# Expert outputs of the first token block brought forward into the input stage, with a weight table for each token block and four places for v's halves

## The reference

```
q = x @ wq; s1, s2 = q_half1 . subkeys1, q_half2 . subkeys2
v1, i1 = top_k(s1, 16);  v2, i2 = top_k(s2, 16)
vals, pos = top_k(v1[:, None] + v2[None, :], 16)
ids = i1[pos // 16] * 128 + i2[pos % 16];  g = softmax(vals)
a = x . u_tab[ids];  y = sum over heads and k of gelu(a) * g * v_tab[ids]
x = LayerNorm(alpha * x + y)
```

## Time and profile before

| | |
|---|---|
| runs (3) | 1092.28 to 1094.7 us, median 1093.67 |
| the profiled execution | 1090.26 us |
| its span | 1088.3 us |
| PE busy | 1021.7 us (94%), 6826 instructions |
| DVE / ACT / POOL busy | 838.3 (77%) / 451.0 (41%) / 451.5 (41%) us |
| DMA | 210.41 MB, 193 GB/s over the span |

### The profile page before, as it was taken

The page is one execution under the profiler, slowest core; times in us unless marked ns, Lnnn a source line. Parts: engine busy times, 40 slices in busy tenths (PEclk is TensorE's granted clock), DMA queues, the critical chain, the costliest instruction groups (busy, mean ns, idle before and its releaser), DMA issues.

```text
span 1088.3 us, 20500 instructions
## 1 busy us (share of the span) xinstructions
PE 1021.7 (94%) x6826; PEld 937.8 (86%) x6826; DVE 838.3 (77%) x1484; ACT 451.0 (41%) x648; POOL 451.5 (41%) x332
## 2 busy tenths in 40 slices
PE   7999999899999999999999999139999999999995
PEld 7878898899999999999999999128888888888884
DVE  3476457778999998988888887038888888888887
ACT  4374444344443334444444444014444444444442
POOL 5800000058888888788888888830000000000000
PEclk9999999999999999999999999559999999999998
DMA  9676688545666667877787775247777777777773
GB/s 305 240 271 224 208 294 295 180 117 117 141 145 141 136 136 164 195 167 170 164 174 168 170 172 99 0 125 238 243 241 241 240 242 240 241 241 241 240 240 128
DMA packets 146735, 210.41 MB, mean 193 GB/s; under 512 B 47376, under 2 KB 95312, under 8 KB 146704
## 3 DMA queue, kind: packets, MB, share of 16 engines
q1 hardware_dynamic: 109264, 208.58, 61.0%
q0 software_dynamic: 37440, 1.43, 10.1%
HBM read 192.00 MB, written 17.96 MB: 193 GB/s over the span
## 4 chain that ended last, share of the span: by engine, by line
PE 47%; POOL 38%; issue 8%; DVE 3%; DMA 2%; ACT 1%; SPq 0%; POOLq 0%; DVEq 0%; ACTq 0%
POOL expert_weights L459 38%; PE ps L1283 32%; PE ps L1200 13%; DMA w_raw<-in_w_in_dram 1%; DVE w_lo L904 1%; ACT w_hi L577 1%; PE ps L1096 1%; PE ps L1074 1%; DVE xres L703 0%; DVE xres L710 0%; PE ps L1084 0%; DMA expert_weights<-gw,cell 0%; DVE small L691 0%; DVE v_lo L984 0%; PE ps L1107 0%
## 5 line engine op out<-in xcount | busy, mean ns | idle before, releaser
L459 POOL DMA_INDIRECT expert_weights<-gw,cell x256 | 411.8, 1609 | 256.4 <-DVE gw L897 175.8
L1241 PE MATMUL ps<-act_hi,uT_hi 128*128 128x256 f32 x1024 | 295.1, 288 | 0.0
L1241 PE MATMUL ps<-act_hi,uT_lo 128*128 128x256 f32 x1024 | 289.9, 283 | 0.0
L1241 PE MATMUL ps<-act_lo,uT_hi 128*128 128x256 f32 x1024 | 289.7, 283 | 0.0
L657 ACT ACTIVATE v_hi<-v_raw 128x512 fp32r<-128x512 f32 x256 | 147.9, 626 | 244.3 <-PE ps L1283 198.5
L1283 PE MATMUL ps<-v_hi,hid_hi 128*128 128x512 f32 x512 | 158.8, 391 | 43.8 <-DVE v_lo L984 43.8
L1241 PEld LDWEIGHTS ps<-act_lo,uT_hi 128*128 128x128 f32 x1024 | 196.6, 192 | 0.0
L1241 PEld LDWEIGHTS ps<-act_hi,uT_hi 128*128 128x128 f32 x1024 | 196.6, 192 | 0.0
L1241 PEld LDWEIGHTS ps<-act_hi,uT_lo 128*128 128x128 f32 x1024 | 196.3, 192 | 0.0
L984 DVE TENSOR_TENSOR v_lo<-v_raw,v_hi 128x512 fp32r<-128x512 f32 x256 | 165.0, 686 | 0.0
L1283 PE MATMUL ps<-v_hi,hid_lo 128*128 128x512 f32 x512 | 158.1, 390 | 0.0
(11 more groups left out here) (151 smaller groups left out, 1397.9 us busy)
## 6 DMA issues: line engine op xcount, KB each, us to landing
v_raw<-in_peer_v_dram SPq DMA_DIRECT2D x128, 512.0 KB, 4.2
u_raw<-in_peer_u_dram SPq DMA_DIRECT2D x68, 512.0 KB
u_raw<-in_peer_u_dram SPq DMA_DIRECT2D x240, 128.0 KB
w_raw<-in_w_in_dram SPq DMA_DIRECT2D x8, 2048.0 KB, 9.5
...
g_in<-expert_weights SPq DMA_DIRECT2D x128, 128.0 KB, 3.0
w_raw<-in_peer_wq_dram SPq DMA_DIRECT2D x4, 2048.0 KB, 10.6
...
```

The lines of the kernel that those rows point to most:

```text
L459: pool.indirect_dma_start(out=table_cells, out_offset=bass.IndirectOffsetOnAxis(ap=cell[:, t, k:k + 1], axis=0), in_=gw[:, t, k:k + 1], in ...
L1241: ins = pe.matmul(ps[:, bank, 0:T], (uT_hi, uT_hi, uT_lo)[part][:, slot, k, :], (act_hi, act_lo, act_hi)[part][:, k, :], start=(k == 0 and ...
```

## The change

- The table is stored as two tables, one for each token block, each with 128 columns. `column` carries the offset of the second. A gate load of both token blocks now reads 256 rows of 512 bytes, where before it read 128 rows of 1 KB.
- The last routing batch (heads 4 to 7) is split into heads 4 and 5, and heads 6 and 7.
- POOL's scatters follow `ORDER`: token block 0 is brought forward, with 4 scatters of token block 1 between its heads (8 after head 7), and then heads 3 to 7 of token block 1 follow each other directly. The rule on earlier heads is unchanged.
- In input rounds 10 to 17 PE adds, after each of the first three blocks' inputs, the token block 0 outputs of one of the expert blocks 104 to 127 (a "fill"): two float32 matmuls of 512 columns, without a split. SP loads its gates (64 KB) and v (512 KB), from round 10 on, after it has waited for all scatters of token block 0. DVE multiplies the gates by H.
- In the output stage the blocks stand in 32 groups of four. In 24 of them the fourth block is one of 104 to 127, for token block 1 alone (6 matmuls, and `hidden` on 128 columns). The other 8 groups are whole. The v of a filled block is loaded a second time.
- `v_hi` and `v_lo` have four places. DVE does `rest_v` two blocks ahead: after `hidden` of block m comes `rest_v` of m + 2, and `rest_v` of blocks 0 and 1 comes ahead of `hidden` of block 0. ACT's rounding waits for block m - 4. SP's order is unchanged: after `hid_done` of m the gates of m + 2, then the v of m + 4.

The diff, cut to its core:

```diff
@@ -36,6 +36,12 @@
 GROUP = 4
 ROUNDS = (NB - NPRE) // GROUP
 BODY = 4
+AHEAD = 2
+FILLS = 24
+FILL_BLOCK = NB - FILLS
+PER_ROUND = 3
+FILL_ROUND = 10
+FILL_END = FILL_ROUND + FILLS // PER_ROUND
...
-BATCHES = ((0, 1, 0, 1), (1, 2, 0, 1), (0, 2, 1, 2), (0, 2, 2, 4), (0, 2, 4, 8))
+BATCHES = ((0, 1, 0, 1), (1, 2, 0, 1), (0, 2, 1, 2), (0, 2, 2, 4), (0, 2, 4, 6), (0, 2, 6, 8))
 EARLY = len(ROUTE_AT)
-MOST_HEADS = 4
+ORDER = [(0, 0, 0, 16), (1, 0, 0, 16), (0, 1, 0, 16), (1, 1, 0, 4), (0, 2, 0, 16), (1, 1, 4, 8), (0, 3, 0, 16),
+         (1, 1, 8, 12), (0, 4, 0, 16), (1, 1, 12, 16), (0, 5, 0, 16), (1, 2, 0, 4), (0, 6, 0, 16), (1, 2, 4, 8),
+         (0, 7, 0, 16), (1, 2, 8, 16)] + [(1, h, 0, 16) for h in range(3, PH)]
+MOST_HEADS = 2
...
-    v_hi = sb("v_hi", [P, 2, D], 169 * K1, F32R)
-    v_lo = sb("v_lo", [P, 2, D], 185 * K1, F32R)
+    v_hi = sb("v_hi", [P, BODY, D], 169 * K1, F32R)
+    v_lo = sb("v_lo", [P, BODY, D], 185 * K1, F32R)
...
+    v_fill = [sb(f"v_fill{n}", [P, D], at * K1) for n, at in enumerate((203, 125, 121))]
+    g_fill = [sb("g_fill0", [P, P], 201 * K1), sb("g_fill1", [P, P], 202 * K1), iota]
...
+    weights = nc.dram_tensor("expert_weights", (TB, NB * P, P), F32)
...
+    table_cells = table_flat.unsqueeze(1)
...
-            sp.dma_start(g_in[:, slot, :], table[bass.ds(b * P, P), :]).then_inc(s[f"g_in{slot}"], 16)
+            sp.dma_start(g_in[:, slot, :].rearrange("p (t c) -> p t c", t=TB),
+                         table[:, bass.ds(b * P, P), :].rearrange("t e c -> e t c")).then_inc(s[f"g_in{slot}"], 16)
+        def load_g_second(b, slot):
+            sp.dma_start(g_in[:, slot, P:T], table[1, bass.ds(b * P, P), :]).then_inc(s[f"g_in{slot}"], 16)
+        def load_fill(f, slot):
+            b = f + FILL_BLOCK
+            sp.dma_start(g_fill[slot][:], table[0, bass.ds(b * P, P), :]).then_inc(s[f"g_fill_in{slot}"], 16)
+            sp.dma_start(v_fill[slot][:], v_dram[bass.ds(b * P, P), :]).then_inc(s[f"v_fill_in{slot}"], 16)
...
+        def next_round(i, begin=False, refill=False):
             sp.wait_ge(s["u_read"], i + (NPRE + 1))
             load_u(GROUP * i + block_of(NPRE + GROUP), 0)
+            if begin:
+                sp.wait_ge(s["scattered0"], 16 * SLOTS)
+                for k in range(PER_ROUND):
+                    load_fill(k, k)
             for k in range(1, GROUP):
+                for place in (((), (0, 1), (2,), ())[k] if refill else ()):
+                    f = PER_ROUND * i + (place - PER_ROUND * FILL_ROUND)
+                    sp.wait_ge(s["fill_done"], f + (1 - PER_ROUND))
+                    load_fill(f, place)
                 sp.wait_ge(s["u_turned"], (GROUP - 1) * i + k)
                 load_u_squares(GROUP * i + block_of(NPRE + GROUP + k), k)
+        with sp.Fori(0, FILL_ROUND) as i:
+            next_round(i)
+        next_round(FILL_ROUND, begin=True)
+        with sp.Fori(FILL_ROUND + 1, FILL_END) as i:
+            next_round(i, refill=True)
+        for i in range(FILL_END, ROUNDS - 1):
+            next_round(i)
         sp.wait_ge(s["u_read"], NPRE + ROUNDS)
         load_v(0, 0)
+        sp.wait_ge(s["fill_done"], FILLS)
         for t in range(TB):
             sp.wait_ge(s[f"scattered{t}"], 16 * SLOTS)
         for b in range(2):
             load_g(b, b)
         for k in range(1, GROUP):
             sp.wait_ge(s["u_turned"], (GROUP - 1) * (ROUNDS - 1) + k)
-            load_v(k, k)
-        with sp.Fori(0, NB // BODY - 1) as i:
...
+        def next_inputs(i, g_blocks, v_blocks):
             for k in range(BODY):
                 sp.wait_ge(s["hid_done"], BODY * i + (k + 1))
-                load_g(BODY * i + (k + 2), k % 2)
+                (load_g_second if k == 1 and g_blocks is mixed else load_g)(g_blocks(i, k + 2), k % 2)
                 sp.wait_ge(s["v_lo_done"], 2 * BODY * i + 2 * (k + 1))
-                load_v(BODY * i + (k + 4), k)
+                load_v(v_blocks(i, k + 4), k)
+        def mixed(i, k):
+            return i + FILL_BLOCK if k == 3 else i + (FILL_BLOCK + 1) if k == 7 else 3 * i + (k if k < 4 else k - 1)
+        def whole(i, k):
+            return BODY * i + (k - FILLS)
+        with sp.Fori(0, FILLS - 1) as i:
+            next_inputs(i, mixed, mixed)
+        next_inputs(FILLS - 1, mixed, whole)
+        with sp.Fori(FILLS, NB // BODY - 1) as i:
+            next_inputs(i, whole, whole)
         for k in range(2):
             sp.wait_ge(s["hid_done"], NB - BODY + k + 1)
-            load_g(NB - BODY + k + 2, k)
+            load_g(FILL_BLOCK - BODY + k + 2, k)
...
-        for h in range(PH):
-            for t in range(TB):
-                for n, (t0, t1, h0, h1) in enumerate(BATCHES):
-                    if (h, t) == (h0, t0):
-                        pool.wait_ge(s["route_done"], n + 1)
-                if h:
...
-                    pool.wait_ge(s[f"scattered{t}"], 16 * TOPK * h)
-                for k in range(h * TOPK, (h + 1) * TOPK):
...
+        for t, h, k0, k1 in ORDER:
+            for n, (t0, t1, h0, h1) in enumerate(BATCHES):
+                if h == h0 and t == t0 and k0 == 0:
+                    pool.wait_ge(s["route_done"], n + 1)
+            if h and k0 == 0:
+                pool.wait_ge(s[f"scattered{t}"], 16 * TOPK * h)
+            for k in range(h * TOPK + k0, h * TOPK + k1):
...
+        def round_v(m, k, landed):
...
-        for m in range(2, BODY):
-            act.wait_ge(s["y_done"], m - 1)
-            round_v(m % 2, m, 16)
+        for k in range(2, BODY):
+            round_v(k, k, 16)
...
-                act.wait_ge(s["y_done"], BODY * i + (k - 1))
-                round_v(k % 2, k, 16 * i + 16)
+                act.wait_ge(s["y_done"], BODY * i + (k - 3))
+                round_v(BODY * i + k, k, 16 * i + 16)
...
+        def fill_hidden(f, slot, landed):
+            dve.wait_ge(s[f"g_fill_in{slot}"], landed)
+            dve.tensor_tensor(g_fill[slot][:], H[:, bass.ds((f + FILL_BLOCK) * T, P)], g_fill[slot][:], ALU.mult) \
+                .then_inc(s["fill_hid"], 1)
...
+                if k == 1 and last_fill:
+                    fill_hidden(f - 1, 2, landed - 16)
+                if k == 3 and fills:
+                    fill_hidden(f, 0, landed)
                 turn(n + k, k, 16 * NQ * i + (before + 16 * NQ))
                 if k == 1:
                     rest_uT(n, 6, 0)
...
+            if fills:
+                fill_hidden(f + 1, 1, landed)
             rest_turned(n + (GROUP - 1), GROUP - 1)
...
+        with dve.Fori(0, FILL_ROUND) as i:
+            main_round(i)
+        main_round(FILL_ROUND, fills=True)
+        with dve.Fori(FILL_ROUND + 1, FILL_END) as i:
+            main_round(i, True, True)
+        main_round(FILL_END, last_fill=True)
+        for i in range(FILL_END + 1, ROUNDS):
+            main_round(i)
...
+        def four(i, head, mixed, ahead=4):
+            for k in range(BODY):
+                b = BODY * i + (k - FILLS) if not mixed else 3 * i + k if k < 3 else i + FILL_BLOCK
+                hidden(BODY * i + k, b, k % 2, 32 * i + 16 * (k // 2 + 1), head and k < 2, mixed and k == 3)
+                if k < ahead:
+                    rest_v(BODY * i + (k + AHEAD), (k + AHEAD) % BODY)
...
+        dve.wait_ge(s["fill_done"], FILLS)
         dve.wait_ge(s["act_done"], NPRE // 2 + BODY)
-        for m in range(BODY):
-            hidden(m, m % 2, 16 * (m // 2 + 1), m < 2)
-            rest_v(m, m % 2, m)
+        for m in range(AHEAD):
+            rest_v(m, m)
+        four(0, True, True)
         dve.wait_ge(s["act_done"], NB)
-        with dve.Fori(1, NB // BODY) as i:
-            for k in range(BODY):
-                m = BODY * i + k
-                hidden(m, k % 2, 32 * i + 16 * (k // 2 + 1), False)
-                rest_v(m, k % 2, k)
+        with dve.Fori(1, FILLS) as i:
+            four(i, False, True)
+        with dve.Fori(FILLS, NB // BODY - 1) as i:
+            four(i, False, False)
+        four(NB // BODY - 1, False, False, BODY - AHEAD)
...
+        def fill(f, slot, landed, opens):
+            pe.wait_ge(s["fill_hid"], f + 1)
+            pe.wait_ge(s[f"v_fill_in{slot}"], landed)
+            for d in range(2):
+                ins = pe.matmul(ps[:, d, :], g_fill[slot][:], v_fill[slot][:, d * 512:(d + 1) * 512],
+                                start=opens, stop=False, skip_group_check=True)
+            ins.then_inc(s["fill_done"], 1)
...
+                if fills and k < PER_ROUND:
+                    fill(PER_ROUND * i + (k - PER_ROUND * FILL_ROUND), k, 16 * i + (16 - 16 * FILL_ROUND),
+                         opens and k == 0)
+        with pe.Fori(0, FILL_ROUND) as i:
             main_four(i, False)
-        main_four(ROUNDS - 1, True)
-        def expert_outputs(slot, t, opens, closes):
+        main_four(FILL_ROUND, False, True, True)
+        with pe.Fori(FILL_ROUND + 1, FILL_END) as i:
+            main_four(i, False, True)
+        for i in range(FILL_END, ROUNDS):
+            main_four(i, i == ROUNDS - 1)
```

(15 more changed lines are left out.)

82 lines of the change are left out of this document (38 added, 44 removed).

## The result

The changed kernel is slower: 1132.7 us (median of 4 runs, 1125.1 to 1141.7) against 1093.9 (1092.3 to 1094.7), a ratio of 1.037 (95% interval 1.033 to 1.040). The profiled execution took 1127.91, span 1126.1, which is 37.8 us above the span before. The forecast of 1103 was too low, and the result lies above the range, which ended at 1120.

A forecast was written before the change was run, and what follows sets the result against it. Scatters and then the output stage were taken to bound the kernel in series: 1090.3 + 16.7 (0.6 + 12.5 + 3.6, later outputs) - 6.7 (output stage) = 1100.3, plus 3 for a median, 1103; range 1076 to 1120.

The forecast's parts named there:

- the loop in the output stage: From hid_done of m over v's load to hid_done of m + 3: 8.0 us for three blocks, 10.7 a four.
- What bounds the kernel: Two stretches in series: 256 scatters taking 490.93 us, then an output stage of about 350 us; PE's idle is slack.
- Fills on PE: Input stage: 24 fills at 1.8 us add 43 us, inputs end at 726.5, before the scatters' end, so costed at nothing.
- Scatters: POOL: 0.6 for an earlier wait plus five landing waits of 2.5 us each; last scatter starts 13.1 later, at 731.6.
- Start of the outputs: Last scatter to first output: DVE's first hidden stands behind rest_v of block 1, so 11.3 us, 3.6 later than now.
- The output stage: PE alone would take 9.52 a mixed four, but the loop holds it to 10.6 against 10.88; gain 6.7 us.
- Landings grow: Rival: v lands in 4.8 us, mixed fours 11.2 and whole 11.3, total +29, 1122; chance 0.13.
- The first rival, PE binding: Output stage: v lands within 3.4 us, so PE sets 9.52 a four; -15.9, so 1078; chance 0.25.
- The scatters hardly stall: Rival: POOL prepares the next scatter during the wait, so PE's inputs and fills bind; -2.5, 1091; chance 0.1.
- The move doesn't bring the fills forward: Rival: token block 0 completes after round 10, u's loads are held and PE stops in the input stage; 1105 to 1115; chance 0.05.

The follow-up runs named there:

- d_fills_no_pe: Changed kernel with no loads for fills 4 to 24 and one PE matmul of 8 columns for each instead of two of 512; 1117.8 us, ratio 1.021.
- the order alone: Kernel before with only the new scatter order and the split routing batch, one table, no fills, old output stage; 1105.1 us, ratio 1.011.
- c_after_again: The changed kernel unchanged, executed and traced once more; 1131.2 us in a single execution.
- a_ahead_only: Kernel before with only four places for v_hi and v_lo and rest_v two blocks ahead, no fills, whole fours; 1103.3 us, ratio 1.011.
- a_v_first: Changed kernel with SP issuing the v of block m + 4 ahead of the wait for hid_done of m; 1110.7 us, ratio 1.019.
- b_deep_gates: Changed kernel with v issued first, first v loads ahead of the scatter wait, and four gate places loaded four blocks ahead; 1086.8 us, ratio 0.993.

## Why the prediction was wrong, step by step

Two steps failed. The first is the sum of the loop in the output stage: 8.0 us for three blocks, against 8.3 measured in mixed fours and 8.7 in whole ones. The loop was seen rightly and its terms were sized too small, by more than the margin on which the gain stood. The second is the cost of the fills, put at nothing: PE's longer rounds went into the scatters, for which the sum had no term.

- **What bounds the kernel: right.** Two stretches in series, scatters and outputs. All of the 37.8 us came out of them and the piece between.
- **Fills on PE: the work right, the cost wrong.** 24 fills end the inputs at 724.2 (last start 723.9) instead of 683.3, so 40.9 us or 1.70 a fill (1.8 was taken), four instructions each. They are hidden as PE work: PE still waits 32 us. But "I cost it at nothing" was wrong in another place, the scatters: 6 to 8 us, by d_fills_no_pe. The step took the longer rounds only as a question of PE's end and did not ask what they do to POOL.
- **Scatters: +13.1 predicted, +25.6 measured.** The wait count was right, and with the order alone so was the price (11.6 against 12.5), partly by luck. The release was taken at 0.88, from a wait for DVE, and a wait for a landing shows 0.27; the landings were taken at 3.5 (2.5 with 1.85 less 0.88) and were 3.9 on average. The two errors nearly cancel. The lower bound of 2.1 us a wait was too high for the same reason, since the last one, on quiet queues, cost 1.4. Of the missing 12.5, 3.5 are longer waits (16.0 against the 12.5 taken), and about 9 are steps without a wait and the gap (14.3 against 4.0 before), a term the sum did not have at all. The range for the waits ended at 18.5, which they kept; the range for the scatters had no room for the rest. The step took POOL's steps without a wait as fixed, though no row shows them under longer rounds.
- **Start of the outputs: nearly right.** 11.3 predicted, 12.15 measured. v was issued 4.1 after the last scatter's start, as said, but was there for ACT 4.9 later (748.23 to 753.13) where 4.0 was taken from the earlier trace rows, beside the gates' short rows.
- **The output stage: right loop, wrong sign.** Predicted -6.7, measured +7.6 (+3.6 in c_after_again). Here is the loop in the changed kernel's timeline, from `hid_done` of one block to that of the third behind it, the one of half size:

```profile
900.14 0.43 DVE L1080 TENSOR_TENSOR hid_lo<-g_in,hid_hi 128x256 fp32r<-128x256 f32 x1
...
900.76 0.38 SPq L355 DMA_DIRECT2D g_in<-expert_weights  x1
...
901.45 0.33 SPq L352 DMA_DIRECT2D v_raw<-in_peer_v_dram  x1
...
905.69 1.15 ACT L713 ACTIVATE v_hi<-v_raw 128x512 fp32r<-128x512 f32 x2 [2.22 <-DMA v_raw<-in_peer_v_dram]
...
906.36 1.29 DVE L1064 TENSOR_TENSOR v_lo<-v_raw,v_hi 128x512 fp32r<-128x512 f32 x2 [0.46 <-ACT v_hi L713]
...
908.15 0.29 DVE L1080 TENSOR_TENSOR hid_lo<-g_in,hid_hi 128x128 fp32r<-128x128 f32 x1
```

  Release 0.19, to v's issue 0.69 (0.50 was taken), to ACT's start 4.24, to v_lo 0.67, v_lo and the half `hidden` 2.08: 7.87 us, close to the prediction's 8.0. In this one pass the sum is nearly right. On average it isn't: 11.07 a four is 8.3 for three blocks. The same terms, as means over all passes of the changed kernel's trace:

  | term | taken | 800 to 1000 (72 passes) | whole fours (24 passes) |
  |---|---|---|---|
  | release, to the gates' issue | 0.17 | 0.18 | 0.18 |
  | to v's issue | 0.50 | 0.64 | 0.70 |
  | to ACT's start | 4.3 | 4.41 | 4.61 |
  | to v_lo | 0.7 | 0.69 | 0.72 |
  | v_lo, to `hidden` | 1.21 | 1.24 | 1.29 |
  | `hidden` | 1.13 | 1.14 (0.87 if half) | 1.23 |
  | sum | 8.0 | 8.30 | 8.73 |

  The 0.50 was the distance of two like issues; from the gates' issue to v's it is 0.61 even with rows of 1 KB (a_ahead_only). The 1.13 left out the end of `hidden`'s last instruction (a whole `hidden` takes 1.2). No single term carries the difference: it is 0.14 at the issues, 0.1 at v's load and 0.1 at `hidden`, and in the whole fours 0.3 at v's load. The landings between 800 and 1000, v's and then the gates', spread widely:

```profile
DMA to landing us min/median/max: 3.4/4.4/5.0
DMA to landing us min/median/max: 2.1/3.7/4.4
```

  Before, v's ran from 4.0 to 4.6 in the same stretch and the gates' from 2.8 to 3.4. With gates and v requested 0.7 apart both spread, but the loop takes in the mean of v's, only 0.1 above the 4.3 taken, and it hardly waits for the gates (2.3 us in 8 waits over the whole stage). That the distance of the loads sets the pace is shown by a_v_first (10.6) and b_deep_gates (9.50). The gain of 0.28 a four stood on a margin of 0.2 us in three blocks (8.0 against PE's 8.16), and four small terms used it up. The whole fours, which the prediction kept at 10.88 since 10.7 "stays below", lost 0.7 each here and 0.2 in c_after_again (11.6 and 11.1).
- In sum the forecast had +10.0 over the profiled execution and it is +37.6: 12.5 of the missing 27.6 are scatters, 0.8 the start, 14.3 the output stage.
- **The rivals.** "Landings grow" came nearest by its numbers for the loop (11.2 and 11.3 a four, a loss of 12 in the stage against 7.6 measured), with 13 in 100; the median landing grew by 0.2, not by 0.5. The first rival, PE binding, needed v within 3.4 us, the least seen here and not the rule; b_deep_gates shows that it is reached by issuing earlier, at any landing seen. "The scatters hardly stall" was wrong in the opposite direction. "The move doesn't bring the fills forward" did not come about: PE is busy for all of 560 to 724. The range left out the upper ends of two costs at once, the scatters and the loop.
- **The Trainium skill** ("DMA: Bandwidth & Descriptors", anatomy of one DMA) gives, for the GpSimd path, an estimate of 3.2 us for 512 KB; v is loaded by SP. This case's median landings are 4.4 to 4.6 in the steady stage at 231 to 268 GB/s, so the measured row decides, as the prediction had it. Of the same page's section on queues and completion order it said that a small rise of the scatter's landing is in agreement. The chains show landings of 3.0 to 4.6 us in the order alone, up to 6.4 in the changed kernel and 7.8 in c_after_again, against 3.06 on idle queues. The rise is not small there.
